# Moving the split of expert weights off GpSimd in the last expert stage, and one v unit in four in full precision

## What is computed

```
def blk(args):
    hx, e, gt = args
    act = jax.nn.gelu(jnp.einsum('nd,nhkd->nhk', hx, expert_u[e]), approximate=False)
    return jnp.einsum('nhk,nhkd->nd', gt * act, expert_v[e])
```

## Time and profile before

| | before |
|---|---|
| median of 3 runs | 3581.2 us (3579.43 to 3587.63) |
| profiled execution: time, span | 3584.34 us, 3582.6 us |
| granted TensorE clock, mean | 0.974 |
| TensorE busy | 3364.7 us (94%) |
| weight loads | 2841.7 us (79%) |
| VectorE busy | 2500.4 us (70%) |
| ScalarE busy | 1687.9 us (47%) |
| GpSimd busy | 1146.6 us (32%) |

### The profile page before, as it was taken

The page is one execution under the profiler, slowest core; times in us unless marked ns, Lnnn a source line. Parts: engine busy times, 40 slices in busy tenths (PEclk is TensorE's granted clock), DMA queues, the critical chain, the costliest instruction groups (busy, mean ns, idle before and its releaser), DMA issues. The chain is left out here.

```text
span 3582.6 us, 51470 instructions
## 1 busy us (share of the span) xinstructions
PE 3364.7 (94%) x20290; PEld 2841.7 (79%) x20290; DVE 2500.4 (70%) x2870; ACT 1687.9 (47%) x2597; POOL 1146.6 (32%) x647
## 2 busy tenths in 40 slices
PE   8999999999999999689988888887999999999999
PEld 7777777788999999689966666666788877788887
DVE  4876766655664785469887888878688886465454
ACT  5653444344444664224434444443665554444763
POOL 0000000000698666872356665555022220000000
PEclk9999999999999999889999999999999999999999
DMA  6654444555565545457767666766543435455344
GB/s 236 209 187 140 169 162 140 218 190 211 178 205 198 186 149 200 153 196 282 268 262 256 248 250 254 255 253 233 183 146 144 147 147 189 176 193 188 141 153 165
DMA packets 148865, 703.80 MB, mean 196 GB/s; under 512 B 34156, under 2 KB 56460, under 8 KB 69946
## 3 DMA queue, kind: packets, MB, share of 16 engines
q1 hardware_dynamic: 121816, 622.99, 48.0%
q0 software_dynamic: 26864, 78.38, 6.4%
HBM read 743.29 MB, written 23.63 MB: 214 GB/s over the span
## 5 line engine op out<-in xcount | busy, mean ns | idle before, releaser
L237 DVE TENSOR_TENSOR lo_w<-ring,hi_w 128x1024 fp32r<-128x1024 f32 x412 | 561.0, 1362 | 592.2 <-ACT hi_w L231 581.2
L231 ACT CAST hi_w<-ring 128x1024 fp32r<-128x1024 f32 x540 | 565.5, 1047 | 814.5 <-DMA ring<-in_wstream 789.9
L2095 PE MATMUL PS<-both_x,hi_w 128*128 128x256 f32 x4096 | 746.5, 284 | 51.7 <-DVE lo_w L239 47.6
L2095 PEld LDWEIGHTS PS<-both_x,hi_w 128*128 128x128 f32 x4096 | 643.0, 192 | 54.9 <-issue 38.8
L2095 PE MATMUL PS<-both_x,lo_w 128*128 128x256 f32 x2048 | 584.9, 286 | 0.0
L232 ACT CAST hi_w<-ring 128x1024 fp32r<-128x1024 f32 x540 | 564.4, 1045 | 0.0
L239 DVE TENSOR_TENSOR lo_w<-ring,hi_w 128x1024 fp32r<-128x1024 f32 x412 | 509.3, 1236 | 0.0
L654 PE MATMUL PS<-hi_w,both_x 128*128 128x512 f32 (+2 forms) x1520 | 499.7, 398 | 5.5 <-DVE RKV L1666 3.2
L237 POOL TENSOR_TENSOR lo_w<-ring,hi_w 128x1024 fp32r<-128x1024 f32 x128 | 345.6, 2700 | 367.5 <-ACT hi_w L231 365.4
L2114 PE MATMUL PS<-hi_w,hi_g 128*128 128x512 f32 x768 | 332.5, 433 | 122.0 <-DVE lo_g L2517 111.4
L2801 PE MATMUL PS<-hi_w,both_x 128*128 128x512 f32 x1232 | 399.9, 400 | 3.9 <-DVE x L3169 1.7
(11 more groups left out here) (588 smaller groups left out, 5328.4 us busy)
## 6 DMA issues: line engine op xcount, KB each, us to landing
ring<-in_wstream SPq DMA_DIRECT2D x540, 1024.0 KB, 4.9
act_dram<-act_early SPq DMA_DIRECT2D x40, 128.0 KB, 4.8
gates_dram<-gst POOLq DMA_DIRECT2D x8, 512.0 KB, 4.3
other_G<-staged SPq DMA_DIRECT2D x16, 256.0 KB, 2.4
R<-act_dram SPq DMA_DIRECT2D x64, 64.0 KB, 6.9
both_x<-other_G SPq DMA_DIRECT2D x1, 4096.0 KB, 15.5
act_dram<-act_late SPq DMA_DIRECT2D x24, 128.0 KB, 2.0
prev<-RKV POOLq DMA_DIRECT2D x6, 508.0 KB, 5.4
```

The costliest lines, as they stand in the source:

```text
L231: a.copy(hi_w[s][:, 0:HALF], ring[s][:, 0:HALF]).then_inc(S(f"hi{s}"), 1)
L237: v.tensor_tensor(lo_w[s][:, 0:HALF], ring[s][:, 0:HALF], hi_w[s][:, 0:HALF].bitcast(F32), ALU.subtract)
L2095: m = nc.tensor.matmul(PS[:, s, 0:T], wa[s][:, k * P:(k + 1) * P], xa[:, k, :], start=(k == 0 and p == 0), stop=(k == KC - 1 and p == 2))
```

## The change

Five edits, all in the expert layer. (1) In v GpSimd splits nothing; VectorE makes all low splits there. (2) The sparse units with p divisible by 4 (p = 8 to 124, 30 of the 64, all in ring slot 0) are not split: TensorE multiplies them in full precision straight from `ring` with `act_b`, and ScalarE and VectorE only pass the semaphores on. (3) Of the 128 cell transfers GpSimd issues 32 at the start of `u_a` instead of 64, and then 2 with each tick from tick 12 instead of 4 from tick 10; `weigh` stands at ticks 13, 36, 52 and in v at p = 5, instead of 9, 12, 36, 38. (4) The row additions start at tick 14 instead of 10, so 50 instead of 54 of them lie in `u_a` and 78 instead of 74 in v. (5) TensorE's loop over v has a body of 12 units instead of 4.

```diff
+def v_whole(p):
+    return v_expert(p)[0] and p % 4 == 0
...
-    ADD0, ADDS_U = 10, HK - 10
+    ADD0, ADDS_U = 14, HK - 14
...
+            def v_whole_half(g, s, k, last=False):
+                t.wait_ge(S(f"landed{s}"), g * 16 + (GROUP["v"] * 16 + 16))
+                t.wait_ge(S("g_lo"), g * 4 + (s + 1))
+                for c in range(4):
+                    m = nc.tensor.matmul(PS[:, c, :], act_b[:, k % AHEAD, :], ring[s][:, c * 512:(c + 1) * 512],
+                                         start=False, stop=last)
+                    if last and c < 3:
+                        m.then_inc(S("v_bank"), 1)
+                m.then_inc(S("unit_used"), 1)
...
             def hi(w):
-                if w < 4 * HK + SLOTS:
+                if VB <= w < 2 * VB and v_whole(w - VB):
+                    a.wait_ge(S(f"landed{w % SLOTS}"), (W0 + w) // SLOTS * 16 + 16)
+                    a.drain().then_inc(S(f"hi{w % SLOTS}"), 2)
+                elif w < 2 * VB + SLOTS:
                     split_hi(a, (W0 + w) // SLOTS, w % SLOTS)
...
@@ GpSimd
-            for s in range(2 * CELLS):
+            for s in range(CELLS):
                 cell(s)
-            for i in range(ADD0, HK):
+            for i in range(ADD0 - 2, HK):
                 for s in fetches(i):
                     fetch(s)
-                at = 2 * CELLS + 4 * (i - ADD0)
-                for s in range(at, min(at + 4, PK)):
+                at = CELLS + 2 * (i - ADD0 + 2)
+                for s in range(at, min(at + 2, PK)):
                     cell(s)
-            lo(VB)
-            lo(VB + 2)
             for p in range(VB):
                 for s in fetches(HK + p):
                     fetch(s)
-                if p % 2 and p + SLOTS - 1 < VB:
-                    lo(VB + p + SLOTS - 1)
@@ VectorE
-                if HK <= w < VB or VB <= w < 2 * VB and w % 2 or 2 * VB <= w < 2 * VB + SLOTS:
+                if VB <= w < 2 * VB and v_whole(w - VB):
+                    v.wait_ge(S(f"hi{w % SLOTS}"), (W0 + w) // SLOTS * 2 + 2)
+                    v.drain().then_inc(S(f"lo{w % SLOTS}"), 1)
+                elif HK <= w < 2 * VB + SLOTS:
                     split_lo(v, (W0 + w) // SLOTS, w % SLOTS)
...
-                if i in (9, 12, 36, 38):
-                    weigh((9, 12, 36, 38).index(i))
+                if i in (ADD0 - 1, 36, 52):
+                    weigh((ADD0 - 1, 36, 52).index(i))
...
             times_a(HK - 1)
             v.drain()
+            lo(VB + 2)
...
+                if p == 5:
+                    weigh(3)
```

More of the change, by code:

```diff
@@ L2223, in _, with v_unit @@
                     u_unit(g, s, 1)
-            for p in range(2 * SLOTS):
[L2225 to L2230, removed]
+            def v_unit(g, p, **mark):
+                sparse, k = v_expert(p)
+                if v_whole(p):
+                    v_whole_half(g, p % SLOTS, k, **mark)
+                else:
+                    (v_half if sparse else v_dense)(g, p % SLOTS, **mark)
+            ROUND, TAIL = 3 * SLOTS, 3 * SLOTS
+            for p in range(2 * SLOTS):
+                v_unit(p // SLOTS, p, **({"first": True} if p == 0 else {}))
+            with t.Fori(0, (VB - TAIL - 2 * SLOTS) // ROUND) as n:
+                for i in range(ROUND):
+                    v_unit(n * 3 + (2 + i // SLOTS), 2 * SLOTS + i)
+            for p in range(VB - TAIL, VB):
+                v_unit(p // SLOTS, p, **({"last": True} if p in (LAST_A, LAST_V) else {}))
             def turn_next(c):
@@ L2270, in high @@
                 sparse, k = v_expert(p)
+                if v_whole(p):
+                    a.wait_ge(S("unit_used"), W0 + VB + p - 3)
+                    a.drain().then_inc(S("g_hi"), 1)
+                    return
                 if p < SLOTS:
@@ L2515, in low @@
                 v.wait_ge(S("g_hi"), p + 1)
+                if v_whole(p):
+                    v.drain().then_inc(S("g_lo"), 1)
+                    return
                 src, w = (act_b[:, k % AHEAD, :], P) if sparse else (GG[:, k, :], T)
```

## The result

| | before | after |
|---|---|---|
| median | 3583.14 us (3579.43 to 3587.63, 4 runs) | 3409.57 us (3405.14 to 3412.41, 4 runs) |
| ratio | | 0.9514, 95% interval 0.9497 to 0.953 |
| profiled execution: time, span | 3584.34, 3582.6 us | 3405.14, 3403.4 us |
| granted TensorE clock, mean | 0.974 | 0.995 |

The changed kernel is 4.9% faster; 3389 us were predicted, 20 us (0.6%) less than it takes, with a range of 3357 to 3448.

A forecast was written before the change was run, and what follows sets the result against it. Bound: late rows from GpSimd's transfers in u's second half; in v, VectorE stretched by GpSimd's splits. 3584.3 - 60 - 127 - 5 = 3392 us profiled, median 3.1 us lower: 3389 us, range 3357 to 3448.

The forecast's parts named there:

- Term 1: Second half of u: spreading the cells removes nearly all of 64 us lost there; -60 us, bounds 45 and 64.
- The first cells are no obstacle: Start of u's second half: 38 cells at 1.3 us take 49 us of GpSimd from 1371 us on, without harm.
- Term 2: v's 28 rounds: each falls from 22.63 to 18.1 us; -127 us, bounds -149 and -88.
- TensorE's need of 17.3 us a round: v: products of three split units plus 3.4 us for a whole unit make TensorE's round 17.3 us.
- The transfers' 15.8 us of work a round: v: the 16 transfer engines are busy 15.8 us a round, under 17.3.
- The chain 12.3 + L: v, dense unit's slot: unit, refill landing (L, taken as 6.0 us), copy, split, addition, small operations, before TensorE's next start there.
- the stalls left are under 1 us each: v: with rounds taken at 18.1 us, TensorE's remaining stalls are each under 1 us.
- Term 3: Start and last seven units of v: VectorE's `lo_g` no longer held by GpSimd; -5 us, bounds 0 and two holds.
- Transfers bind: v: transfers go no denser and set the round, 88 us or less gained there; 3428 to 3456 us, chance 0.17.
- GpSimd starves the additions: Second half of u: additions hold GpSimd's transfers, ticks of 7.6 us lose 48 us; 3437 us, chance 0.08.
- VectorE's order: v: VectorE's waits for ScalarE's copy delay queued work, round 18.5 us; 3400 us, inside the forecast, no chance of its own.
- Slower by the clock: v: full-precision products don't count as work, TensorE falls to 1.2 GHz; +266 us, about 3787 us, chance 0.02.

The follow-up runs named there:

- cells only: Kernel before with only cells spread, additions from tick 14 and later weigh ticks; GpSimd still splits v's even units, no unit whole: ratio 0.9821, 3554.39 us.
- the block of 64: Changed kernel with 64 instead of 32 cells issued ahead of the first row fetches, still two a tick: 3421.26 us, ratio 0.9551.
- changed, again: The changed kernel itself, unaltered, timed once more on another chip against the kernel before: 3409.58 us, ratio 0.9505.
- low first: Changed kernel with VectorE making `low` right behind the low split, ahead of the row addition: ratio 0.9413, and 0.9398 (3366.58 us) when run again.

## Why the prediction was right

**What bounds the kernel: right in both places.** In u, GpSimd's rate (four cells a tick brings the waits back); in v, VectorE held by GpSimd's splits (one split in four brings 5 us holds back, and 28 us).

**Term 1, -60 us: measured -63.8** in the trace, and 64 by the ratio of cells only. Three transfers in 5.69 us are stable, five are not. "The first cells are no obstacle" held for the 38 of the change. Its 1.3 us a cell was too little, 1.45 us was measured even with no addition beside; with the block of 64 the fourth row came 11.6 us after it was due.

**Term 2, -127 us: measured -105.0.** This is the term that was mis-sized, by 22 us; terms 1 and 3 gave about 10 us more than forecast. In the profiled executions the miss is 13 us (3392 forecast, 3405.14 measured). The other 7 us of the 20 are no mechanism: the prediction put the median 3.1 us below the profiled execution, and it lies 4.4 us above. Its parts: TensorE's need of 17.3 us a round was right, the undisturbed rounds take 17.3 to 17.6; a whole unit takes 3.45 us (3.4 by the earlier trace rows). The transfers' 15.8 us of work a round was right, 0.84 x 18.88 = 15.9. The chain 12.3 + L was right in every link. Wrong was to take one L of 6.0 us from the DMA share and to write that "the stalls left are under 1 us each". The 54 refills of dense slots issued and used within these rounds take 4.6 to 8.0 us. Their mean, 5.8 us, is even under the 6.0, but a mean was the wrong number to put in: with an addition in the chain each refill over 5 us makes a stall, and one under 5 gives nothing back. An estimate from the single refills bears this out. The chain of each (12.3 + L, or 2.46 less where no addition lies in it), never under 17.3 us, and in each round the longer of its two, comes to 18.8 us a round; forecast were 18.1, measured 18.88 (for the execution of changed, again it comes to 19.0, measured 19.25). The lower clock, which the forecast left out of its 18.1, is a small part of this, 7 us in 28 rounds.

What makes a refill late is shown only in part. Without row fetches in v nearly all land after 4.8 us. With one or more of them in flight a refill of the changed kernel takes anything from 4.6 to 9.0 us, and the kernel before has row fetches too, and a median of 4.9 us at its lower DMA share.

By the Trainium skill (FP8 and Floating Point Precision, TensorE Precision Notes), with four passes for a true fp32 product, the whole unit would have taken 3.7 us, an estimate. It took 3.45 us; the row was the better source. That doesn't speak against four passes, only against pricing each at a whole product's 0.2316 us: it would be 0.216 us.

**Term 3, -5 us: measured about -11**, at the edge of its bounds of 0 to 11: 1.8 at v's head, and 9.2 from the gate load of unit 120 to v's last product (35.4 us before, 26.2 now). The rest of the program then took 1.4 us more, which makes the 7.8 above.

**The rivals.** Transfers bind: shown wrong, v runs at a DMA share of 0.88 to 0.89 with rounds at 17.6 to 18.1 us as soon as the addition is out of the chain. GpSimd starves the additions: not at three transfers a tick. The Trainium skill (GPSIMD Engine Reference, Key points) has GpSimd and VectorE share their SBUF interfaces, with contention for VectorE instructions with two SBUF inputs. The traces agree: GpSimd's `tensor_tensor` holds a VectorE operation of 0.29 us for 5.25 us, and a transfer issued beside an addition is held until behind it. But the hold is not the same for every such instruction: beside a low split a transfer takes little longer (1.61 us in the rows of the 64 cells, where one alone takes 1.00). VectorE's order: the prediction put this at nothing outside the forecast; it is what was left to win, 1.0% to 1.1%. Slower by the clock: wrong, the whole units ran at the upper clock level (8 records in 3.45 us), and the mean in v is 0.98.

The prediction never asked what edit (2), the units in full precision, is worth alone. Its worth can't be told from nothing in either order of work. It takes 2.3 us of split off VectorE and puts 0.67 us on TensorE, while what set the rounds was a chain through the dense units' slots, which the edit doesn't touch; only where that chain is cut does VectorE come into sight as the bound (384 of 400 us), and there what it saves and what it adds nearly cancel. That last step is argued from the busy times, not tested by itself.

Left open: in the four traces of the chip at 3617.13 us the 64 activations of the second half of u take 29 to 42 us longer than the 358.4 of the changed kernel, nearly all of it between about 1375 and 1437 us. TensorE stops there again and again with no releaser in the profile ("issue"), and transfers stand nearly still (DMA share 0.02 from 1390 to 1400 us in two of them). No other trace has it, and no run was made to settle it. The kernel before was 34 us slower on that chip too, but no profile shows whether for this reason; low first came to 0.9413 there and to 0.9398 on another chip, so the ratios of that set are hardly touched by it.

## What to carry to other kernels

When a chain through a buffer's refill is close to the round's length, don't put a mean landing time into it: stalls come from the late refills and the early ones don't pay them back. Ask what the clock does, too: behind some stalls the products ran at the lower level, which was some 43 of the 105 us won in v. An instruction that nobody waits for soon (an addition) should stand behind the small ones that TensorE waits for, not ahead of them; that cost nothing and was worth a fifth of what the whole change was here. And when a change has several edits, cost each one alone: one of them may carry nothing.

## What the runs showed of the hardware

A VectorE operation of 0.29 us beside the two halves of a GpSimd `tensor_tensor` split (2.41 and 2.40 us) ended only after both of them, 5.25 us after its start: the second half, issued later, went ahead of it as well.

Refills of 1 MB land after 4.8 us (median) with no row fetches beside them at a DMA share of 0.69, after 4.9 us with row fetches at the same share (the kernel before), after 5.8 us at 0.84 and after 6.7 us at 0.88; most of TensorE's rounds were the shortest (17.3 to 17.5 us) both at 4.8 and at 6.7 us.

A stall of 2.6 us at clock 1.00 was followed, 1.3 us after TensorE went on, by eight products 0.42 us apart, the spacing of 1.2 GHz, before they were back at 0.23. Four idle spells of 2.3 to 2.9 us in the 28 rounds were followed by such a spell, five of 2.1 to 2.5 us were not.
